# Mixer projections as three fp32r products of parted weights, and the first tile of a wide expert in plain fp32

## The chip, the cores and the metric

The kernel runs on one core of a Trainium2 chip. The metric is the device time of one execution in microseconds, lower is better; a time given for the kernel is the median of its runs. A core has TensorE (PE, matrix products), VectorE (DVE), ScalarE (ACT), GpSimd (POOL) and SyncE (SP), each with a queue of its own that is worked off in order, and 16 DMA engines that they share.

## The reference

Two layers over 256 tokens of width 1024, all in fp32. Each layer has two sub-layers, and each of these is a norm with a modulation by the condition vector (shift, scale and gate, three rows of 1024, from `silu(c) @ w_ada`), the sub-layer itself, a second norm, and the gated addition to x.

```python
h = rmsnorm(x, g_norm[l, 0]) * (1.0 + scale) + shift
# hybrid_mixer: one input projection, three head groups, one output projection
(q1, q2, k1, k2, va, qb, kb, vb, ob, ib, fb, cq, ckv, kr) = split(h @ w_in)      # 1024 x 2668
out_a = diff_attention_group(q1, q2, k1, k2, va, ...)                           # 4 heads
out_b = mlstm_group(qb, kb, vb, ob, ib, fb, ...)                                # 6 heads
out_c = mla_group(cq, ckv, kr, ...)                                             # 6 heads
y = concatenate([out_a, out_b, out_c]) @ w_out                                  # 1024 x 1024
x = x + gate * rmsnorm(y, g_norm[l, 1])
...
# layer 0: dense SwiGLU of width 3584; layer 1: 8 experts of that width, each token goes to 2
y = (silu(h @ w_gate) * (h @ w_up)) @ w_down
```

## The kernel before

It is written as one instruction stream for each engine, with semaphores between them by hand; nothing is scheduled by a planner. The stages are mixer 0, dense MLP, mixer 1, and the eight experts one after another.

**Weights.** All weights but the experts' stand in one list, `weight_uses()`, in the order of use: for each mixer 12 input projection items (`W_IN_ORDER`: two for the latents of group c with the gates, then a0, a1, va, qk0, qk1, qk2, ob0, ob1, and two for vb), thirds of a modulation as four quarters each (`ADA_MIXER`), and four output projection items (`OUT_ORDER`, columns 2, 3, 0, 1). A use is up to 1 MB, 128 partitions by 2048 elements. SyncE loads use u (L756) into slot u mod 7 of `ring`, and waits for that with the last reader of use u-7 (`last_reader`), so at most seven uses are in flight or in use. TensorE waits for the landing.

**Mixer on TensorE.** Every input projection is a plain fp32 product, of h (`hT`, feature-major) with the landed weight: `fm_pair` (L949) makes two feature-major banks of 128 rows by 256 tokens with 16 products of 256 columns, `tm` (L957) makes the token-major latents, va and vb. `ada_rows` (L866) multiplies a third's four quarters with the condition vector in 32 products, and waits for all four; `ada_columns` (L877) turns the result. Between the projections stand the attention units. Behind vb come, in this order: the turns `pt`, the modulation rows of the mixer's second last third, the gates (L1144), mt0, the pairs of units w and s of the mLSTM group (L1162, L1170; ScalarE takes the exponential of w, VectorE multiplies), co (L1185), bo (L1199), mt1 and mt2, the output projection's early feature tiles (L1211, `MIX_EARLY`) for two column groups, the modulation rows of the last third, mt3 and mt4, and the rest of the output projection. All of it takes its mixed rows from `mixT`.

**Dense MLP and experts.** These use three fp32r products in place of one fp32 product: the weight's high part (ScalarE Copy to fp32r, `parts<-ring`), its low part (VectorE, weight minus high part), and the same for h; high x high, high x low and low x high are added up in PSUM. Experts have a ring of their own of 14 slots of 1 MB (SyncE, L762), 42 uses each. An expert's code is chosen by its count of rows: up to 64 narrow (plain fp32, L1370 and L1382), 128 split, 160 or 192 wide. Here two are wide, one of 160 and one of 192 rows. `expert_wide` has 14 stages; a stage multiplies two inner tiles' gate and up weights in two halves (`gate_up_half`: L1414 with high weights and high and low rows side by side, L1420 with low weights), adds and multiplies them on ScalarE and VectorE (L2403, L2406), and a stage later the down projection (L1433, L1442). ScalarE copies the high parts of the first weights once it has the expert (L1563, `scr_parts<-ring`); VectorE makes the rows' high and low part (L2392, L2394) and the weights' low parts (L2365).

All ScalarE instructions are recorded under the one helper line, L1563.

Of the kernel before, what the change touches and what calls it, by code (L numbers as in the profile page):

```python
# [24 lines left out]
P = 128  # L25
# [91 lines left out]
def weight_uses():  # L117
# [6 lines left out]
    def w_in(l, a, b):  # L124
        uses.extend(("in", l, key) for key in W_IN_ORDER[a:b])

    def mixer(l):
# [6 lines left out]
        uses.extend(("out", l, c) for c in OUT_ORDER)  # L134
# [27 lines left out]
def pack_weights(inputs):  # L162

    def cols(w, c, n):
        return w[:, c:c + n].reshape(KD, P, n).transpose(1, 0, 2).reshape(-1)
# [5 lines left out]
    for kind, a, b in weight_uses():  # L171
        if kind == "ada":
            parts.append(cols(inputs["w_ada"][a // 2, a % 2], b * SW, SW))
        elif kind == "in":
# [10 lines left out]
def pack_experts(inputs):  # L185
# [15 lines left out]
W_IN_ORDER = [(COL_LAT, 256), (COL_LAT + 256, LATW - 256), (COL_Q, 256), (COL_Q + 256, 256), (COL_VA, 256),  # L201
              (COL_QK, 256), (COL_QK + 256, 256), (COL_QK + 512, 256), (COL_OB, 256), (COL_OB + 256, 128),
              (COL_VB, 256), (COL_VB + 256, 128)]
# [20 lines left out]
            *[f"pt{u}" for u in range(6)], "rows2", "gt", "mt0", "cols2", "co0", "co1", "mt1", "mt2", "rows3",  # L224
# [64 lines left out]
def build(nc, ap, out, ypairs):  # L289
# [13 lines left out]
    with ExitStack() as ctx:  # L303
# [172 lines left out]
        yeK = hT.rearrange("p k t -> p (k t)").rearrange("p (b d) -> p b d", b=TB)  # L476
        htok_hi, htok_lo = (h_parts[:, i, :, :].rearrange("p k t -> p (k t)").rearrange("p (b d) -> p b d", b=TB) for i in range(2))
# [81 lines left out]
        tok_ready = sem("tok_ready")  # L559
        split_hi = sem("split_hi")  # L560
# [66 lines left out]
        def use_wait(eng, u):  # L627

            eng.wait_ge(landed[slot_of[u]], 16 * (u // SLOTS + 1))
# [98 lines left out]
        def _(sp):  # L728
            def last_reader(kind, a, b):

                if kind == "ada":
                    return tr_full, TR.full(("ada", a, b // 4))
                if kind == "in":
                    return pj_full, PJ.full((IN_ITEM[b], a))
                if kind == "out":
                    return (y_full, 2 + a) if b == OUT_ORDER[-1] else (out_read, (D // SW - 1) * a + OUT_ORDER.index(b) + 1)
                return split_lo, dense_use(kind, b) + 1

# [4 lines left out]
            for u, (kind, a, b) in enumerate(uses):  # L743
                if u >= SLOTS:
                    sp.wait_ge(*last_reader(*uses[u - SLOTS]))
                n = KD * (b[1] if kind == "in" else SW)
                slot = ring[:, slot_of[u], :, :]
                if n < KD * SW:
                    slot = slot[:, :, 0:n // KD]
# [45 lines left out]
        def _(pe):  # L795
# [605 lines left out]
            def expert_wide(e, n):  # L1401
# [55 lines left out]
                for s in range(STAGES + 1):  # L1457
# [4 lines left out]
                    if s:  # L1462
                        down_rest(s - 1)
# [1131 lines left out]
```

## Time and profile before

| | |
|---|---|
| median of 3 runs | 1719.91 us (1714.5 to 1721.17) |
| profiled execution | 1717.92 us |
| its span | 1716.1 us |
| mean granted TensorE clock | 0.95 |
| TensorE busy | 1512.4 us, 88% |
| VectorE busy | 732.0 us, 43% |
| ScalarE busy | 561.5 us, 33% |
| GpSimd busy | 63.2 us, 4% |
| bytes moved | 488.85 MB, 285 GB/s |

The span is what the profile shows from first to last instruction; the time has 1.8 us more around it. TensorE busy includes time in which it works at half its clock. The mixers stand at about 28 to 216 and 481 to 667 us, the dense MLP between them, the experts from about 706 on.

### The profile page before, as it was taken

The numbers are of one execution on the slowest core, as the hardware profiler recorded it, in microseconds if no ns is written. First come the engines' busy times: TensorE is split into PE (matmuls) and PEld (weight loads), VectorE is DVE, ScalarE is ACT, GpSimd is POOL, SyncE is SP. The second block draws the span as 40 slices with busy tenths as digits, with TensorE's granted clock in tenths as the row PEclk, the third lists the DMA queues.
The fourth block names the chain that finished last, engine by engine and source line by source line (L and its number), as shares of the span: only waits on it lengthen the run. The fifth ranks groups of instructions, "written<-read, shape, count | busy, mean of one in ns | idle before, by whom it ended". The sixth has DMA issues, their size and how long they took to land.

```text
span 1716.1 us, 29819 instructions
## 1 busy us (share of the span) xinstructions
PE 1512.4 (88%) x12054; PEld 1200.4 (70%) x12055; DVE 732.0 (43%) x1058; ACT 561.5 (33%) x777; POOL 63.2 (4%) x66
## 2 busy tenths in 40 slices
PE   5999999999999999856659999989997669999894
PEld 3868878999976776644447875489995458888552
DVE  2263265565534522300018871166772036666212
ACT  2134144444322321100016751056551035554101
POOL 0010000000010001000000000000000000000002
PEclk9999999999999999987879999989999779999997
DMA  9726467545352436699999999997577996555793
GB/s 357 273 95 239 191 245 276 201 176 203 138 192 74 173 147 274 273 424 423 425 425 426 400 378 403 425 369 286 236 279 313 424 424 260 221 221 221 311 426 149
DMA packets 74557, 488.85 MB, mean 285 GB/s; under 512 B 9792, under 2 KB 13920, under 8 KB 16544
## 3 DMA queue, kind: packets, MB, share of 16 engines
q1 hardware_dynamic: 72176, 479.94, 69.7%
q10 hardware_dynamic: 1648, 4.59, 0.8%
q8 instruction: 114, 1.87, 0.4%
q0 software_dynamic: 576, 2.10, 0.4%
q14 instruction: 43, 0.35, 0.1%
HBM read 482.66 MB, written 3.93 MB: 284 GB/s over the span
## 4 chain that ended last, share of the span: by engine, by line
PE 79%; DMA 10%; issue 5%; DVE 3%; ACT 2%; POOL 1%; SPq 1%; ACTq 0%; POOLq 0%; DVEq 0%
PE PG L1370 9%; PE PG L923 6%; PE Y L949 5%; PE PG L1414 5%; PE PG L1480 5%; PE TRB L1414 4%; DMA arena<-in_experts 4%; PE Y L1382 4%; PE Y L1442 4%; DMA ring<-in_experts 4%; PE Y L1211 3%; PE Y L957 3%; PE PG L925 3%; PE TRB L1420 3%; PE PG L1420 3%
## 5 line engine op out<-in xcount | busy, mean ns | idle before, releaser
L1370 PE MATMUL PG<-ring,mixT 128*32 128x128 f32 (+1 forms) x1920 | 116.3, 347 | 61.4 <-issue 56.9
L2381 DVE COPY arena<-TRB 128x64 f32<-128x64 f32 (+1 forms) x70 | 17.6, 251 | 340.3 <-PE TRB L1356 340.3
L1563 ACT ACTIVATE parts<-ring 128x2048 fp32r<-128x2048 f32 x84 | 157.2, 1901 | 4.8 <-PE PG L1480 4.8
L923 PE MATMUL PG<-h_parts,parts 128*128 128x512 f32 x432 | 152.8, 394 | 1.4 <-DVE arena L2260 1.4
L1370 PEld LDWEIGHTS PG<-ring,mixT 128*32 128x32 f32 (+1 forms) x1920 | 89.5, 136 | 91.7 <-issue 77.0
L1563 ACT ACTIVATE rope<-PG 64x128 f32<-64x128 f32 (+2 forms) x84 | 27.2, 324 | 376.5 <-PE PG L1370 352.6
L1370 PE MATMUL PG<-arena,mixT 128*32 128x128 f32 (+1 forms) x1664 | 103.6, 357 | 41.3 <-issue 41.3
L1370 PEld LDWEIGHTS PG<-arena,mixT 128*32 128x32 f32 (+1 forms) x1664 | 79.8, 141 | 69.1 <-issue 55.1
L925 PE MATMUL PG<-h_parts,parts 128*128 128x256 f32 x432 | 121.8, 282 | 0.0
L2245 DVE TENSOR_TENSOR parts<-ring,parts 128x2048 fp32r<-128x2048 f32 x42 | 95.1, 2289 | 32.7 <-ACT parts L1563 32.7
L2365 DVE TENSOR_TENSOR ring_parts<-ring,parts 128x2048 fp32r<-128x2048 f32 x42 | 95.0, 2286 | 22.4 <-PE Y L1433 19.4
L2365 DVE TENSOR_TENSOR parts<-arena,parts 128x2048 fp32r<-128x2048 f32 x42 | 95.2, 2287 | 17.6 <-PE Y L1433 14.9
L923 PEld LDWEIGHTS PG<-h_parts,parts 128*128 128x128 f32 x432 | 81.2, 188 | 19.4 <-DVE arena L2260 1.6
L949 PE MATMUL Y<-hT,ring 128*128 128x256 f32 x416 | 93.2, 384 | 0.0
L949 PEld LDWEIGHTS Y<-hT,ring 128*128 128x128 f32 x416 | 79.4, 193 | 11.6 <-issue 0.8
L925 PEld LDWEIGHTS PG<-h_parts,parts 128*128 128x128 f32 x432 | 81.3, 188 | 0.0
L1563 ACT ACTIVATE parts<-arena 128x2048 fp32r<-128x2048 f32 x42 | 78.9, 1901 | 3.6 <-PE PG L1480 3.6
L890 PE MATMUL Y<-parts 128*128 128x256 f32 x224 | 63.4, 283 | 0.2 <-DVE parts L2269 0.2
L892 PE MATMUL Y<-parts 128*128 128x256 f32 x224 | 63.4, 283 | 0.0
L891 PE MATMUL Y<-parts 128*128 128x256 f32 x224 | 63.4, 283 | 0.0
L1414 PEld LDWEIGHTS PG<-h_parts,scr_parts 128*128 128x128 f32 x224 | 37.3, 198 | 36.3 <-ACT scr_parts L1563 20.4
L1414 PE MATMUL PG<-h_parts,scr_parts 128*128 128x320 f32 (+1 forms) x224 | 45.7, 348 | 19.0 <-ACT scr_parts L1563 19.0
(358 smaller groups left out, 2715.6 us busy)
## 6 DMA issues: line engine op xcount, KB each, us to landing
ring<-in_experts SPq DMA_DIRECT2D x168, 1024.0 KB, 12.2
arena<-in_experts SPq DMA_DIRECT2D x168, 1024.0 KB, 16.3
ring<-in_weights SPq DMA_DIRECT2D x116, 1024.0 KB, 6.3
ring<-in_weights SPq DMA_DIRECT2D x4, 512.0 KB, 4.2
ypairs<-hT ACTq DMA_DIRECT2D x3, 512.0 KB, 5.4
tok<-in_x SPq DMA_DIRECT2D x1, 1024.0 KB, 9.0
result<-scr SPq DMA_DIRECT2D x2, 512.0 KB, 2.6
ring<-in_weights SPq DMA_DIRECT2D x2, 432.0 KB, 6.5
```

The lines of the kernel that those rows point to most:

```text
L923: mm(PG[:, m, :].rearrange("p (i t) -> p i t", i=2), w_hi[d % SPLITS][:, c], h_parts[:, :, k, :], start=(k == 0), stop=False, skip_group_c ...
L925: last = mm(PG[:, m, 0:T], w_lo[d % SPLITS][:, c], h_hi[:, k, :], start=False, stop=(k == KD - 1), skip_group_check=True)
L949: last = mm(bank_part, ring[:, s, k, c:c + m], hT[:, k, :], start=(k == 0), stop=(k == KD - 1))
L1370: last = mm(bank[i * n:(i + 1) * n, 0:width], xe[:, k, 0:n], w[k // 4][:, k % 4, i * width:(i + 1) * width], start=(k == 0), stop=(k == KD ...
L1382: last = mm(o, actT[:, s % 2, f, 0:n], w[:, f, c:c + width], start=(s == 0 and f == 0), stop=(s == STAGES - 1 and f == 1))
L1414: last = mm(both, hi[:, k, i // 2, i % 2, :], h_parts[:, :, h * KD // 2 + k, 0:n], start=(h == 0 and k == 0), stop=False, skip_group_check ...
L1420: last = mm(bank[:, 0:n], lo[:, k, i // 2, i % 2, :], h_parts[:, 0, h * KD // 2 + k, 0:n], start=False, stop=(h == 1 and k == KD // 2 - 1) ...
L1442: last = mm(o, a[:, s % 2, f, :], w[:, f, c:c + width], start=(opens and s == 0 and f == 0), stop=(closes and s == STAGES - 1 and f == 1))
L1480: last = mm(bank, x[j][:, h * KD // 2 + k, :], w[:, k, :], start=(opens and k == 0), stop=(closes and k == KD // 2 - 1))
L1563: return nc.scalar.activation(out_, in_, func, **kw)
L2245: V.tensor_tensor(w_lo[d % SPLITS], ring[:, slot_of[slot_of_dense(d)], :, :].rearrange("p k c -> p (k c)"), w_hi[d % SPLITS].bitcast(F32), ...
L2365: V.tensor_tensor(w_lo_e[q % SLOTS_E], ring_e[q % SLOTS_E].rearrange("p k c -> p (k c)"), w_hi_e[q % HI].bitcast(F32), ALU.subtract).then_ ...
```

## The change

In the mixers every projection weight is now parted: it takes two uses of the ring, the weight itself (`"in"`, `"out"`) and a place for its high part (`"hi"`), for which SyncE issues nothing. ScalarE copies the high part (`part`), VectorE subtracts it from the weight in place (`lower`). h goes to `h_hi`, its low part to `h_lo` (`low_shifted`). TensorE makes three products.

```diff
     def w_in(l, a, b):
-        uses.extend(("in", l, key) for key in W_IN_ORDER[a:b])
+        uses.extend((kind, l, key) for key in W_IN_ORDER[a:b] for kind in ("in", "hi"))
...
-        uses.extend(("out", l, c) for c in OUT_ORDER)
+        uses.extend((kind, l, c) for c in OUT_ORDER for kind in ("out", "hi"))
...
+            def part(l, key):
+                u, n = proj_use(l, key)
+                use_wait(ae, u)
+                if u + 1 >= SLOTS:
+                    ae.wait_ge(*last_reader(*uses[u + 1 - SLOTS]))
+                run(ring_parts[:, slot_of[u + 1], 0:n], ring[:, slot_of[u], :, :].rearrange("p k c -> p (k c)")[:, 0:n],
+                    ACT.Copy).then_inc(proj_hi, 1)
...
+            def lower(l, key):
+                u, n = proj_use(l, key)
+                ve.wait_ge(proj_hi, proj_index(l, key) + 1)
+                V.tensor_tensor(ring_parts[:, slot_of[u], 0:n], ring[:, slot_of[u], :, :].rearrange("p k c -> p (k c)")[:, 0:n],
+                                ring_parts[:, slot_of[u + 1], 0:n].bitcast(F32), ALU.subtract).then_inc(proj_lo, 1)
...
                 def fm_pair(name, key, n=2):
                     bank = take_pj((name, l))
-                    s = slot("in", key)
+                    hi, lo = proj_parts(l, key)
+                    hi_of(key)
                     for i in range(n):
-                        last = fm(bank[:, i * T:(i + 1) * T], s, i * P, P)
+                        for k in range(KD):
+                            for x in (h_hi, h_lo):
+                                mm(bank[:, i * T:(i + 1) * T], hi[:, k, i * P:(i + 1) * P], x[:, k, :],
+                                   start=(i == 0 and k == 0 and x is h_hi), stop=False, skip_group_check=True)
+                    lo_of(key)
+                    for i in range(n):
+                        for k in range(KD):
+                            last = mm(bank[:, i * T:(i + 1) * T], lo[:, k, i * P:(i + 1) * P], h_hi[:, k, :],
+                                      start=False, stop=(k == KD - 1), skip_group_check=True)
                     last.then_inc(pj_full, 1)
```

`latents` does the same for both latent items at once (48 products of 364 columns; each item is now half of the features, not of the columns), `tm` for va (256 columns) and vb (384 columns), `mixed` for the output projection. The mixed rows go to `mix_hi` and `mix_lo`. ScalarE's parts stand by hand between its other work: the first two between the two first modulation thirds, the first output weight's ahead of the w exponentials. The last third's modulation rows move from between the early and late output projection to behind co.

```diff
-                run(mixT[:, 0:2, :], bank.rearrange("p (a t) -> p a t", a=2), ACT.Copy, scale=gd[:, l:l + 1]).then_inc(free, 1)
+                run(mix_hi[:, 0:2, :], bank.rearrange("p (a t) -> p a t", a=2), ACT.Copy,
+                    scale=gd[:, l:l + 1]).then_inc(mix_hi_ready, 1)
+                part(l, OUT_ORDER[0])
                 ae.wait_ge(*tr_done("gt", l))
                 for h in range(BH):
...
             mean("pre", 0)
+            lower(0, W_IN_ORDER[0])
             for third in ADA_START:
                 ada(third)
...
+                part(l, W_IN_ORDER[10])
                 at(2)
                 at(3)
+                part(l, W_IN_ORDER[11])
```

In a wide expert the first stage's gate and up are multiplied in plain fp32 from the landed weights; their conversion is left out, and the rows' low part is made in two halves later.

```diff
+                def gate_up_whole():
+
+                    for h in range(2):
+                        w = landed_unit(e, "gu", 0, h).rearrange("p (k g f c) -> p k f g c", k=KD // 2, g=2, f=2)
+                        for i, bank in enumerate(banks):
+                            for k in range(KD // 2):
+                                last = mm(bank[:, 0:n], w[:, k, i // 2, i % 2, :], xe[:, h * KD // 2 + k, 0:n],
+                                          start=(h == 0 and k == 0), stop=(h == 1 and k == KD // 2 - 1))
+                            if i == 2:
+                                used = last
+                        (used if h else last).then_inc(hi_used, 1)
+                    last.then_inc(gu_full, 2)
...
-                for q in range(HI):
-                    weights_lo(e, q)
+                ve.sem_inc(conv_lo, 2)
+                weights_lo(e, expert_at["gu", 1, 0])
                 for s in range(STAGES):
                     if s == 0:
+                        ve.wait_ge(hi_used, e * USES + 1)
+                        low_rows_of(0)
                         weights_lo(e, expert_at["gu", 1, 1])
```

SyncE's queue in layer 0's mixer, before: the rows from the last vb weight on, each with the kind of reader that it waits for (`pj_full` a projection, `tr_full` modulation rows or turns, `out_read` and `y_full` the output projection).

```order
13 L756 DMA ring<-in_weights 128x8x128 [waits tr_full]
14 L756 DMA ring<-in_weights 128x2048 [waits tr_full] x3
15 L756 DMA ring<-in_weights 128x2048 [waits pj_full] x4
16 L756 DMA ring<-in_weights 128x2048 [waits tr_full] x8
17 L756 DMA ring<-in_weights 128x2048 [waits out_read] x3
18 L756 DMA ring<-in_weights 128x2048 [waits y_full]
```

The same place now, from the two vb halves (128x1536) on:

```order
12 L781 DMA ring<-in_weights 128x1536 [waits tr_full] x2
13 L781 DMA ring<-in_weights 128x2048 [waits pj_full] x7
14 L781 DMA ring<-in_weights 128x2048 [waits tr_full] x5
15 L781 DMA ring<-in_weights 128x2048 [waits out_read] x5
16 L781 DMA ring<-in_weights 128x2048 [waits y_full] x2
```

Before, row 13 is the last vb weight. Three quarters of the modulation third behind vb (row 14) wait for the modulation rows ahead of ob, its fourth for ob0; the next third's first quarter waits for ob1 and the next two for vb (row 15); its last and three output weights wait for the modulation rows behind vb. Now the seven loads behind vb are that third's four quarters and three of the next third's: the first three wait for ob, the other four for vb. The eighth and the first output weight wait for the modulation rows behind vb.

ScalarE in layer 0, before: from the modulation rows behind vb to the first w exponentials (`arena<-PG,aK`).

```order
74 L1563 ACTIVATE arow<-TRB 128x256 [waits tr_full]
75 L1563 ACTIVATE aK<-TRB 128x12 [waits tr_full]
76 L1563 ACTIVATE em<-TRB 128x12
77 L1563 ACTIVATE mixT<-TRB,gd 128x512 [waits tr_full]
78 L1563 ACTIVATE arena<-PG,aK 128x256 [waits sc_full,tr_free1]
79 L1563 ACTIVATE arena<-PG,aK 128x128
```

The same place now:

```order
87 L1653 ACTIVATE arow<-TRB 128x256 [waits tr_full]
88 L1653 ACTIVATE aK<-TRB 128x12 [waits tr_full]
89 L1653 ACTIVATE em<-TRB 128x12
90 L1653 ACTIVATE h_parts<-TRB,gd 128x512 [waits tr_full]
91 L1653 ACTIVATE ring_parts<-ring 128x2048 [waits tr_full,landed6]
92 L1653 ACTIVATE arena<-PG,aK 128x256 [waits sc_full,tr_free1]
93 L1653 ACTIVATE arena<-PG,aK 128x128
```

Row 91 is new: the part of the first output weight, with a wait for its landing (slot 6), ahead of all exponentials.

TensorE at the start of the wide expert of 160 rows, before:

```order
2633 L1456 ISA [waits xe_ready]
2634 L1396 ISA [waits x_split]
2635 L1414 MATMUL PG<-h_parts,scr_parts 128x320 [waits conv_hi]
2636 L1414 MATMUL PG<-h_parts,scr_parts 128x320 x7
2637 L1414 MATMUL TRB<-h_parts,scr_parts 128x320 x8
2638 L1420 MATMUL PG<-h_parts,ring_parts 128x160 [waits conv_lo]
```

The same place now:

```order
2840 L1420 ISA [waits xe_ready]
2841 L1489 MATMUL PG<-mixT,ring 128x160 [waits landed_e0]
2842 L1489 MATMUL PG<-mixT,ring 128x160 x7
2843 L1489 MATMUL TRB<-mixT,ring 128x160 x8
2844 L1489 MATMUL PG<-mixT,ring 128x160 [waits landed_e1]
2845 L1489 MATMUL PG<-mixT,ring 128x160 x7
2846 L1489 MATMUL TRB<-mixT,ring 128x160 x8
2847 L1550 ISA
2848 L1551 ISA [waits act_ready]
2849 L1474 ISA [waits x_split]
2850 L1505 MATMUL PG<-h_parts,parts 128x320 [waits conv_hi]
```

The first products wait for landings where they waited for the conversion (`conv_hi`); the second stage's are the first that need it.

## Rows read from the trace of the kernel before

**Rows 1.** The page, part 4: the chain that ended last, by engine.

```profile
PE 79%; DMA 10%; issue 5%; DVE 3%; ACT 2%; POOL 1%; SPq 1%; ACTq 0%; POOLq 0%; DVEq 0%
```

**Rows 2.** Windows: stretch, us, busy PE PEld DVE ACT POOL, TensorE clock, DMA share, GB/s.

```profile
40.00:216.00 176.00, 171.68 (x1090) 134.26 (x1092) 64.92 (x151) 49.75 (x129) 11.57 (x8) 1.00 0.52 201
1143.00:1290.00 147.00, 147.00 (x1111) 132.79 (x1111) 101.67 (x84) 83.48 (x85) 0.27 (x1) 1.00 0.66 262
1290.00:1375.00 85.00, 57.93 (x1071) 42.92 (x1069) 12.16 (x33) 9.07 (x22) 1.63 (x1) 0.86 0.94 383
```

**Rows 3.** Timeline of layer 0's projections, TensorE: start, busy time, line, operation [idle before].

```profile
40.21 10.70 PE L957 MATMUL Y<-ring,hT 128*128 128x256 f32 x64 [1.38 <-ACT hT L1563]
50.74 13.99 PE L949 MATMUL Y<-hT,ring 128*128 128x256 f32 x64
150.88 5.40 PE L957 MATMUL Y<-ring,hT 128*128 128x256 f32 x32
```

**Rows 4.** Timeline of TensorE in the dense MLP and expert 6: single fp32r products.

```profile
245.69 0.28 PE L890 MATMUL Y<-parts 128*128 128x256 f32 x1
247.95 0.28 PE L891 MATMUL Y<-parts 128*128 128x256 f32 x1
1400.80 1.59 PE L1414 MATMUL PG<-h_parts,parts 128*128 128x384 f32 x8
1402.22 1.57 PE L1414 MATMUL TRB<-h_parts,parts 128*128 128x384 f32 x8
```

**Rows 5.** The page, part 5: turning 128x2048 weights into parts, ScalarE and VectorE.

```profile
L1563 ACT ACTIVATE parts<-ring 128x2048 fp32r<-128x2048 f32 x84 | 157.2, 1901 | 4.8 <-PE PG L1480 4.8
L2245 DVE TENSOR_TENSOR parts<-ring,parts 128x2048 fp32r<-128x2048 f32 x42 | 95.1, 2289 | 32.7 <-ACT parts L1563 32.7
```

**Rows 6.** Timeline of layer 0's mixer behind its last vb projection.

```profile
158.31 3.66 PE L866 MATMUL TRB<-ring,ccol 128*32 128x256 f32 x64
164.05 1.44 ACT L1563 ACTIVATE arena<-PG,aK 128x256 f32<-128x256 f32 x4
170.92 4.13 PE L1185 MATMUL TRB<-arena 128*128 128x64 f32 x36
180.64 8.87 PE L1211 MATMUL Y<-mixT,ring 128*128 128x256 f32 x40 [0.90 <-ACT mixT L1563]
195.16 12.32 PE L1211 MATMUL Y<-mixT,ring 128*128 128x256 f32 x56
215.09 1.38 PE L833 MATMUL TRB<-scr,ones 128*32 128x256 f32 x8
```

**Rows 7.** Tile ring, 156 to 170: the issues, and their time to landing.

```profile
L756 SPq DMA_DIRECT2D ring<-in_weights x6: 327/432/732, 156.3 to 163.4; - x6
DMA to landing us min/median/max: 4.9/7.1/12.3
```

**Rows 8.** Timeline of layer 0's first modulation rows, and a window inside them.

```profile
32.17 5.35 PE L866 MATMUL TRB<-ring,ccol 128*32 128x256 f32 x64 [2.22 <-DMA ring<-in_weights]
33.00:36.00 3.00, 3.00 (x35) 1.91 (x28) 0.00 (x0) 0.00 (x0) 0.00 (x0) 0.50 1.09 343
```

**Rows 9.** Timeline of the first wide expert's start (160 rows), and its first loads.

```profile
1108.32 3.65 PE L1382 MATMUL Y<-arena 128*64 128x512 f32 x16
1117.26 1.91 ACT L1563 ACTIVATE scr_parts<-ring 128x2048 fp32r<-128x2048 f32 x1
1119.22 2.50 PE L1414 MATMUL PG<-h_parts,scr_parts 128*128 128x320 f32 x8 [7.25 <-ACT scr_parts L1563]
1132.33 2.49 PE L1414 MATMUL PG<-h_parts,parts 128*128 128x320 f32 x8 [1.85 <-DVE rope L2403]
ring<-in_experts SPq DMA_DIRECT2D x2, 1024.0 KB, 19.7
```

**Rows 10.** Timeline of the second wide expert's start (192 rows).

```profile
1394.31 2.93 PE L1414 MATMUL PG<-h_parts,scr_parts 128*128 128x384 f32 x8 [11.79 <-ACT scr_parts L1563]
1407.65 2.17 PE L1414 MATMUL PG<-h_parts,parts 128*128 128x384 f32 x8 [2.09 <-DVE rope L2403]
```

More of the change, by code:

```diff
@@ L173, in pack_weights @@
             parts.append(cols(inputs["w_ada"][a // 2, a % 2], b * SW, SW))
+        elif kind == "hi":
+            continue
+        elif kind == "in" and b in K_HALF:
+            at, n, k = K_HALF[b]
+            parts.append(cols(inputs["w_in"][a], at, n, k, KD // 2))
         elif kind == "in":
@@ new lines, in tm @@
+                def tm(bank_part, b, his, los):
+                    for k in range(KD):
+                        nk = KD // len(his)
+                        x_hi, x_lo = (x[:, k, b * P:(b + 1) * P] for x in (h_hi, h_lo))
+                        mm(bank_part, x_hi, his[k // nk][:, k % nk, :], start=(k == 0), stop=False, skip_group_check=True)
+                        mm(bank_part, x_lo, his[k // nk][:, k % nk, :], start=False, stop=False, skip_group_check=True)
+                    for k in range(KD):
+                        last = mm(bank_part, h_hi[:, k, b * P:(b + 1) * P], los[k // nk][:, k % nk, :],
+                                  start=False, stop=(k == KD - 1), skip_group_check=True)
@@ L1014, in mixer @@
                 keys = W_IN_ORDER
-                s0, s1 = slot("in", keys[0]), slot("in", keys[1])
-                for b in range(TB):
-                    bank = take_pj((f"lat{b}", l))
-                    tm(bank[:, 0:SW], s0, b, SW, first=(b == 0))
-                    last = tm(bank[:, SW:LATW], s1, b, LATW - SW)
-                    last.then_inc(pj_full, 1)
+                latents()
                 fm_pair("a0", keys[2])
@@ L1207, in mixed, with product @@
                 def mixed(c, tiles):
-                    s = slot("out", c)
+                    hi, lo = proj_parts(l, c)
+                    late = tiles is MIX_LATE
+                    def product(w, x, k, j):
+                        return mm(Yk[:, 2 * c + j, :], w[:, k, j * P:(j + 1) * P], x[:, k, :],
+                                  start=(j == 0 and k == 0 and w is hi and x is mix_hi),
+                                  stop=(late and k == MIX_LATE[-1] and x is mix_lo), skip_group_check=True)
+                    hi_of(c)
                     for j in range(2):
                         for k in tiles:
-                            last = mm(Yk[:, 2 * c + j, :], ring[:, s, k, j * P:(j + 1) * P], mixT[:, k, :],
-                                      start=(j == 0 and k == 0), stop=(k == MIX_LATE[-1]), skip_group_check=True)
+                            product(hi, mix_hi, k, j)
+                    if not late:
+                        for j in range(2):
+                            for k in tiles:
+                                product(hi, mix_lo, k, j)
+                    lo_of(c)
+                    for j in range(2):
+                        for k in tiles:
+                            last = product(lo, mix_hi, k, j)
+                    if late:
+                        pe.wait_ge(mix_lo_ready, 2 * l + 2)
+                        for j in range(2):
+                            for k in tiles:
+                                last = product(hi, mix_lo, k, j)
                     return last
@@ L1731, in _ @@
             run(cos[CN:CN + CR, :], cos[CN:CN + CR, :], ACT.Sin).then_inc(rope_set, 1)
-            for third in ADA_START:
-                ada_rows(third)
+            ada_rows(ADA_START[0])
+            for key in W_IN_ORDER[0:2]:
+                part(0, key)
+            ada_rows(ADA_START[1])
             shift(0)
@@ L1772, in _ @@
             load_latent_weights(1)
+            for key in W_IN_ORDER[0:2]:
+                part(1, key)
             squares_pre(2)
```

264 lines of the change are left out of this document (181 added, 83 removed).

## The prediction

> **What bounds the kernel now.** I read the chain of waits first, to see on which engine the end hangs, then the windows, since the answer is not the same in every stage. 79% of the chain is TensorE, 10% transfers [rows 1]. In the windows the reader is to see three kinds of stage: layer 0's mixer, where TensorE is busy 171.68 of 176 us with half of the DMA share in use; the first wide expert's stages, busy 147.00 of 147 us; and a narrow expert, 57.93 of 85 us with the DMA engines at 0.94 [rows 2]. Both parts of the change lie on the bound: the projections in the first kind, the start of a wide expert ahead of the second. So TensorE time saved there is time saved at the end, as long as no new wait takes it back.
>
> **The projections, before the last vb (point V).** Four feature-major banks of 16 fp32 products take the 64 matmul records from 50.74 to 64.58 for two pairs, so 13.84/2 = 6.92 us a pair (the busy 13.99 counts a modelled tail), 0.433 a product of 256 columns [rows 3]. An fp32r product of 256 columns costs (247.95 - 245.69)/19 = 0.119 us, one of 384 columns (1402.22 - 1400.80)/8 = 0.178 [rows 4]. Three products in place of one make a pair 48 x 0.119 = 5.71: 1.21 less. There are six such items (a0, a1, va, qk0 to qk2), ob0 as well, ob1 at half, and two vb of 24 x 0.178 = 4.26 against about 5.3 (the row's 5.40 less its tail). Sum: 7 x 1.21 + 0.6 + 2 x 1.05 = 11.2 us a layer. The latents' 10.70 [rows 3] become 48 products of 364 columns, about 0.17 each, the first eight at the pace at which h comes: 0.8 less.
>
> What is added is conversion: every weight is copied on ScalarE (1.90 us) and subtracted on VectorE (2.29 us) [rows 5], 4.2 us behind its landing, and each takes two of the seven slots. Both engines have the room (64.92 and 49.75 us of 176 busy [rows 2]), so I cost most of it at nothing; a pair's 5.71 us on TensorE covers the pair of conversions of the next. Where they stand in line with something urgent they cost: a half of the latents (1456 of 2048 columns, 1.35 us on ScalarE) stands ahead of the copy of the modulation rows, +1.3; at2 and at3 stand behind the part of a vb weight, +1.9; the first vb product waits for its second low part (1.6 on ScalarE, 1.7 on VectorE less what lies beside at and pt), +2.1; pt1, +0.3. V comes 11.2 + 0.8 - 5.6 = 6.4 us earlier in layer 0, I take 6.6 with rounding of the hand walk. In layer 1 the two latent parts stand ahead of squares and means that the norm needs, +2.0, with the rest as above: V 5.6 earlier.
>
> **From V to the end of the output projection (E).** Before, V is about 156.1, the modulation rows of the second third run at 158.31, the first exponentials at 164.05, the c outputs at 170.92, the early part of the output projection at 180.64, the late part at 195.16, E at 215.09: 59.0 us [rows 6]. Here the lookahead decides. The SP order shows that the seven loads ahead of the last third's last quarter wait for projections: the last quarter of that third is now released by V itself, and behind it come the other third's four quarters and the output weights. A lone 1 MB lands 4.9 us after its issue, and a train of them comes at 2.5 us each (the row's 4.9, 7.1, then up to 12.3) [rows 7]. Issued at V they land at V+5.1, 7.6, 10.2, 12.7, then 15.3, and the first output weight, sixth in that train, at V+17.8. ScalarE's order has the high part of that weight ahead of the w exponentials, which before ran at V+7.9. They now start at 17.8 + 1.9 = V+19.8: a block of 11.9 us in which TensorE has next to nothing. w and s take 6.9 (164.05 to 170.92), so c begins at V+26.3, where it was V+14.8; the modulation rows (3.66) and bo follow to V+37.9, the early output part starts at V+40.5 (before V+24.5) and takes 60 x 0.119 = 7.15 for 8.8, since the modulation rows between early and late are gone. The late part has its inputs at V+50.1 and takes (36 + 96) x 0.119 = 15.7, plus 0.6 for the statistics and 1.1 for the low parts of the mixed rows: E = V+67.5, so +8.5 a layer. Bounds of the block: nothing, if the weight were there in time (E = V+55.6, a gain of 3.4), or 14.4 us, if each of the five loads between takes 3 us (12.3 us for the last of a train is the nearest row). I keep 11.9, since the order of the queue leaves little choice.
>
> **The clock.** A pause of 2.22 us ends with a granted clock of 0.50, which is 1.2 of 2.4 GHz, and 64 modulation matmuls that take 3.66 us elsewhere take 5.35: 1.7 us lost a time [rows 6, 8]. The change makes about three such pauses in each layer (before the last quarter, before w, before the output part). The rival price is 0, if TensorE has little to do in that time anyway (w and s are paced by ScalarE and VectorE), the other end 6. I take 4 a layer, 8 in all.
> The Trainium skill speaks against this change here: "TensorE: Matmul & The Clock Gate", section "HAM oscillation — how this bites in real kernels", says that a loop whose bursts of matmuls are parted by waits for transfers pays for the clock anew at every wait. By that rule each of the six pauses costs its 1.7, so 10 in place of my 8, and the forecast 1724. The trace agrees with it for the one pause in front of the modulation rows.
>
> **The wide experts.** Before, TensorE ends the expert before at 1112.0 (1108.32 + 3.65), waits for ScalarE's high part (1117.26 for 1.91) and starts at 1119.22, after 7.25 idle; the second tile starts at 1132.33 [rows 9]. With the landed weights (issued at about 1090, 19.7 to landing, so 1110 and 2 us later) the first tile is 32 fp32 products of 160 columns, 0.433 x 160/256 = 0.270 each, 8.6 us: done at 1120.7, no conversion in front. Then VectorE sets the pace: its own high rows, the low part of the third weight (ScalarE 1117.26 to 1119.15, then 2.29), half the low rows, the low part of the fourth, two copies: 1125.4, where TensorE takes up the second tile. That is 6.9 before 1132.33; I take 6.5. In the second wide expert TensorE comes only at about 1389.9, from fetching its code (11.79 idle up to 1394.31, the rest of it for ScalarE) [rows 10]; 32 x 0.324 = 10.4 plus the slow clock 2, plus copies: 1403.9 for 1407.65, 3.8, and 0.7 for the shorter pause in front of the next tile: 4.5. What is won is kept: the stages behind are TensorE's alone, and the narrow expert's transfers are released by TensorE's progress, so they shift with it. Together -11, between -5 (VectorE's chain longer by two more conversions, the copies behind them) and -16 (no pause at all, full clock).
>
> **Sum** against the profiled execution, 1717.92 us (span 1716.1): -6.6 - 5.6 + 17.0 + 8 - 11 + 0.3 (a third's rows behind the later landing) = +2.1, 1720.0. The median of the runs is 1719.91, 2 us over that execution, so I forecast 1722.
>
> **The rivals.** A, faster: before V the conversions run wholly beside TensorE. For it: the two engines are busy a third of the time, and the ring lets them work a weight ahead [rows 2]; against it: their orders put attention's copies behind parts that wait for a landing. Then V moves by the whole 12.0 in each layer, and fewer pauses leave 4 of the clock's 8: -24 + 17 + 4 - 11 = -14, and 1706. It would be 1683 with the block gone as well, to which I give nothing apart from the range's edge, since the block follows from the queue's order. B, slower: the block, and the clock at 0.50 throughout w, s, c and the early output part. It decides from the point where TensorE's bursts there are too thin to bring the clock back: the 11.9 us block then costs 4 to 5 more a layer (some 9 us of TensorE work at double time, half hidden), and the wide expert's fp32 tile at half clock gives back 6 of the 11. 1722 + 9 + 6 = 1737.
> ScalarE's engine queue is strict first in, first out by the Trainium skill ("TensorE: Matmul & The Clock Gate", section "Architectural detail: the array is 16× 32×32, not 1× 128×128"), so by it nothing behind the waiting part can pass it, and no row here shows a pass.
> C: the experts' part does nothing, since the wide tile's start is bound by the landing and the code fetch: 1722 + 11 = 1733. For it speaks that at the first wide start DMA is full, against it that its weights land before TensorE comes.
>
> **How the numbers follow.** Forecast 0.38 (own range 1712 to 1730), A 0.29, B 0.25, C 0.08. A measurement of this kernel tells 0.5% (8.6 us) from no change. Of the forecast's share a twentieth falls on either side of 1711.3 and 1728.5, and of A's and C's a little within them. Faster 0.29, same 0.37, slower 0.34. The range takes in A's and B's prices: 1701 to 1739.
>
> **What would show it.** In each mixer, an idle of TensorE in front of w of 8 to 12 us, ended by ScalarE, itself waiting for a landing; the c outputs about V+26; the output projection's records at 0.119 us; V at about 149.5 in layer 0; granted clock 0.50 around V+20. For the experts: fp32 records of 160 columns from 1112 on, relative to the end of the expert before, and the next tile 13 us behind. The forecast is wrong if the first output weight lands before V+10, if the low parts (VectorE) hold the pairs before V, or if the windows of w and s show the clock at 1.00.

## The result and the profile after

The changed kernel takes 1729.47 us in the median of 7 runs (1727.48 to 1735.51), beside 1719.39 us for the kernel before: a ratio of 1.0066, 95% interval [1.0049, 1.0083]. It is slower by 0.5 to 0.8%, 8 to 14 us. The profiled execution took 1727.48 us, its span 1725.7 us, 9.6 more than before.

The first view is TensorE's timeline of layer 0's mixer, which answers to [rows 3] and [rows 6]; columns as there.

```profile
41.72 5.52 PE L1001 MATMUL Y<-ring_parts,h_parts 128*128 128x364 f32 x16 [1.39 <-ACT h_parts L1653]
52.30 4.09 PE L979 MATMUL Y<-h_parts,ring_parts 128*128 128x256 f32 x32
...
134.69 4.63 PE L1179 MATMUL TRB<-arena 128*128 128x64 f32 x24 [1.34 <-ACT arena L1653]
...
139.71 0.52 PE L1023 MATMUL Y<-ring_parts,h_parts 128*128 128x384 f32 x1
...
147.82 0.34 PE L1022 MATMUL Y<-ring_parts,h_parts 128*128 128x384 f32 x1
...
152.01 1.30 PE L1069 MATMUL TRB<-con,arena 128*128 128x128 f32 x8
...
157.16 6.42 PE L891 MATMUL TRB<-ring,ccol 128*32 128x256 f32 x64 [2.89 <-DMA ring<-in_weights]
...
173.54 1.65 PE L1221 MATMUL PG<-arena,con 128*128 128x384 f32 x2 [6.36 <-ACT arena L1653]
...
180.38 4.13 PE L1244 MATMUL TRB<-arena 128*128 128x64 f32 x36
...
194.68 7.42 PE L1272 MATMUL Y<-h_parts,ring_parts 128*128 128x256 f32 x60 [1.75 <-DVE h_parts L2306]
...
205.48 10.31 PE L1272 MATMUL Y<-h_parts,ring_parts 128*128 128x256 f32 x84
...
222.23 1.38 PE L858 MATMUL TRB<-scr,ones 128*32 128x256 f32 x8
```

The last vb product ends at 152.0 (V), 4.1 us earlier than before. The reader is to see one bracket ahead of it and three behind. Ahead: 1.34 us for ScalarE in front of at2, then 24 products in 4.63 us, and vb products of 384 columns at 0.32 us from start to start where the later ones take 0.17 (the windows 135 to 139 and 139 to 142 have a granted clock of 0.56 and 0.50). Behind: 2.89 us for the last quarter of a modulation third, whose rows then take 6.42 us in place of 3.66; 6.36 us for ScalarE in front of the second w pair; 1.75 us for VectorE. The output projection ends (E) at 222.2: 70.2 us behind V where it was 59.0. In layer 1 V comes at 611.1 and E at 683.3, 72.2 us:

```profile
596.98 0.66 PE L1022 MATMUL Y<-ring_parts,h_parts 128*128 128x384 f32 x1 [1.69 <-DVE ring_parts L2098]
...
616.22 5.35 PE L891 MATMUL TRB<-ring,ccol 128*32 128x256 f32 x64 [2.86 <-DMA ring<-in_weights]
...
632.78 1.65 PE L1221 MATMUL Y<-arena,con 128*128 128x384 f32 x2 [7.62 <-ACT arena L1653]
...
654.68 8.77 PE L1272 MATMUL Y<-h_parts,ring_parts 128*128 128x256 f32 x60 [1.80 <-DVE h_parts L2306]
```

What ScalarE does in layer 0's pause of 6.36 us stands in its own timeline:

```profile
164.84 0.69 ACT L1653 ACTIVATE h_parts<-TRB,gd 128x512 fp32r<-128x512 f32 x1 [0.63 <-PE TRB L1210]
170.95 1.91 ACT L1653 ACTIVATE ring_parts<-ring 128x2048 fp32r<-128x2048 f32 x1 [5.43 <-DMA ring<-in_weights]
172.77 1.34 ACT L1653 ACTIVATE arena<-PG,aK 128x256 f32<-128x256 f32 x4
```

It waits 5.43 us for the first output weight's landing, copies it, and only then takes the exponentials whose products had stood in PSUM since 165. The windows of the same stretch (stretch, us, busy PE, PEld, DVE, ACT, POOL, granted clock, DMA share, GB/s) show what the pauses do to the clock:

```profile
157.00:164.00 7.00, 6.76 (x68) 3.60 (x68) 0.00 (x0) 0.36 (x2) 0.00 (x0) 0.59 0.96 404
167.00:173.00 6.00, 0.17 (x4) 0.00 (x0) 0.00 (x0) 2.05 (x2) 0.00 (x0) 0.72 0.95 403
173.00:178.00 5.00, 4.46 (x17) 2.75 (x17) 3.68 (x4) 2.57 (x8) 0.00 (x0) 0.65 0.00 0
178.00:192.00 14.00, 14.00 (x152) 11.55 (x151) 4.65 (x9) 3.65 (x6) 0.00 (x0) 1.00 0.21 70
```

The wide experts' starts, which answer to [rows 9, 10], in TensorE's timeline:

```profile
1130.57 2.44 PE L1489 MATMUL PG<-mixT,ring 128*128 128x160 f32 x16 [2.97 <-issue]
...
1141.16 1.44 PE L1505 MATMUL PG<-h_parts,parts 128*128 128x320 f32 x8 [1.64 <-DVE rope L2583]
...
1403.31 5.48 PE L1489 MATMUL PG<-mixT,ring 128*128 128x192 f32 x16 [11.19 <-issue]
```

In the first, the second tile starts at 1141.16. Everything had been moved by 15.6 us there (the last narrow products start at 1123.94, before at 1108.32), so it is 6.8 us earlier than before relative to them. That holds for this execution. In a second profiled one of the same kernel (e10) the pause in front of the first tile is longer and the tile starts at half clock, the second tile starts at 1143.59 with the last narrow products at 1122.11, and only 2.5 us are gained:

```profile
1130.93 4.63 PE L1489 MATMUL PG<-mixT,ring 128*128 128x160 f32 x16 [5.16 <-issue]
```

In the second wide expert TensorE is idle for 11.19 us, and the profile shows nothing that it waits for ("issue"). I read this as the wait for its own code; the runs e6 to e12 bear on that.

GpSimd's copy of each expert's rows marks the experts' starts, so their differences are the time of an expert (us; of the last, up to the copy of the results):

```
                        start e0   e0     e1      e2     e3   e4 wide 160  e5   e6 wide 192  e7
before                    704.1   77.0   107.2   131.1   85.9    184.3    89.0    209.9    100.2
changed                   720.9   77.3   107.2   131.1   84.6    176.1    91.2    209.0    101.1
e1_wide_only              705.9   76.0   106.8   129.9   86.2    177.3    90.2    203.8    100.3
e2_mixer_only             719.9   75.4   108.6   129.9   84.4    181.6    91.5    210.8    100.3
```

So the 9.6 us are: layer 0's mixer +7.1 (the same products of the dense MLP stand at 247.1 for 240.0), layer 1's +9.7, the experts -7.2. One row is one execution: in e10, the changed kernel again, the wide expert of 160 rows takes 180.4 us and not 176.1.

### The profile page after: what moved, and what is told of

Read it like the earlier page. It is cut to its first block, busy times and chain, and to the rows that moved or that the text cites. A ratio compares the mean times of both kernels' runs of the same rounds, so it can differ in the third digit from the quotient of the medians.

```text
span 1725.7 us, 30580 instructions
## 1 busy us (share of the span) xinstructions
PE 1492.7 (86%) x12358; PEld 1197.5 (69%) x12359; DVE 801.1 (46%) x1120; ACT 603.9 (35%) x801; POOL 65.4 (4%) x66
## 4 chain that ended last, share of the span: by engine, by line
PE 44%; DMA 8%; issue 5%; DVE 2%; ACT 1%; POOL 1%; SPq 0%; ACTq 0%; POOLq 0%; DVEq 0%
PE PG L1448 9%; DMA ring<-in_experts 5%; PE PG L1570 5%; PE Y L1460 4%; PE PG L1505 4%; PE Y L1533 4%; PE TRB L1505 4%; PE TRB L1511 3%; PE PG L1511 3%; DMA arena<-in_experts 3%; PE Y L1601 2%; PE Y L1524 2%; PE TRB L1434 2%; PE Y L1272 1%; PE PG L1489 1%
## 5 line engine op out<-in xcount | busy, mean ns | idle before, releaser
L1653 ACT ACTIVATE parts<-ring 128x2048 fp32r<-128x2048 f32 x82 | 153.6, 1901 | 9.4 <-PE PG L1570 4.7
L1448 PE MATMUL PG<-arena,mixT 128*32 128x128 f32 (+1 forms) x1664 | 99.0, 339 | 37.1 <-issue 37.1
L1448 PEld LDWEIGHTS PG<-arena,mixT 128*32 128x32 f32 (+1 forms) x1664 | 75.4, 133 | 65.8 <-issue 51.8
L2536 DVE TENSOR_TENSOR ring_parts<-ring,parts 128x2048 fp32r<-128x2048 f32 x40 | 90.6, 2288 | 25.5 <-PE Y L1524 16.6
L2098 DVE TENSOR_TENSOR ring_parts<-ring,ring_parts 128x2048 fp32r<-128x2048 f32 (+3 forms) x32 | 66.4, 2077 | 37.7 <-ACT ring_parts L1653 37.6
L1653 ACT ACTIVATE ring_parts<-ring 128x2048 fp32r<-128x2048 f32 (+3 forms) x32 | 55.5, 1738 | 57.1 <-DMA ring<-in_weights 30.9
L891 PE MATMUL TRB<-ring,ccol 128*32 128x256 f32 x768 | 52.6, 435 | 10.5 <-DMA ring<-in_weights 10.5
L1460 PE MATMUL Y<-arena 128*32 128x256 f32 (+1 forms) x512 | 59.7, 458 | 1.9 <-issue 1.8
```

The source lines that it names most:

```text
L1448: last = mm(bank[i * n:(i + 1) * n, 0:width], xe[:, k, 0:n], w[k // 4][:, k % 4, i * width:(i + 1) * width], start=(k == 0), stop=(k == KD ...
L1460: last = mm(o, actT[:, s % 2, f, 0:n], w[:, f, c:c + width], start=(s == 0 and f == 0), stop=(s == STAGES - 1 and f == 1))
L1653: return nc.scalar.activation(out_, in_, func, **kw)
L2098: V.tensor_tensor(ring_parts[:, slot_of[u], 0:n], ring[:, slot_of[u], :, :].rearrange("p k c -> p (k c)")[:, 0:n], ring_parts[:, slot_of[u ...
L2536: V.tensor_tensor(w_lo_e[q % SLOTS_E], ring_e[q % SLOTS_E].rearrange("p k c -> p (k c)"), w_hi_e[q % HI].bitcast(F32), ALU.subtract).then_ ...
```

## The experiments

Ratios are to the kernel before on the same chip, with their 95% intervals.

```
kernel                  median us   ratio, interval            V to E, layers 0 and 1
before                  1719.39                                59.0   59.0
changed                 1729.47     1.0066 [1.0049, 1.0083]    70.2   72.2
e1_wide_only            1706.77     0.9936 [0.9920, 0.9951]
e2_mixer_only           1736.55     1.0110 [1.0095, 1.0124]
e3_part_behind          1712.42     0.9962 [0.9949, 0.9976]    63.6   60.9
e4_rows_behind          1701.88     0.9897 [0.9882, 0.9913]    56.9   56.7
e5_tuned                1700.49     0.9889 [0.9869, 0.9910]    57.5   57.3
e6_shift_a (2 runs)     1697.46     0.9877 [0.9848, 0.9905]
e7_shift_b (2 runs)     1698.71     0.9884 [0.9864, 0.9904]
e8_after_shift          1727.96     1.0063 [1.0043, 1.0084]
e9_tuned_shift          1702.39     0.9916 [0.9893, 0.9938]
```

e10, e11 and e12 are the changed kernel, e1 and e9 once more, one execution each: 1731.22, 1709.15 and 1704.00 us, beside one of 1713.28 us for the kernel before.

**e1_wide_only and e2_mixer_only: the two parts of the change, each alone.** e1 has the edits of `expert_wide` on the kernel before, e2 is the changed kernel with `expert_wide` as before. Of e1's edit two lines:

```diff
+                gate_up_whole()
+                for s in range(1, STAGES + 1):
```

> The wide experts' part alone, the mixers as before. Theory 1 (the two parts add up, and the experts' part gains what the two traces show): the span is 7.2 us shorter than before, 8 at the first wide expert, 1 at the second, and 2 of it given back in the narrow one between them: 1711 to 1713 us. Theory 2 (the gain is an accident of when the transfers stand, since the mixers moved all loads by 17 us): anything from 1705, if the second wide expert gains its 4.5, to 1720.

> The mixers' part alone, the experts as before. Theory 1 (parts add up): 7 us in layer 0 and 9.7 in layer 1 more than before, 16.8 in all, 1735 to 1738 us, with all experts later by the same 16.8. Rival: the experts' transfers, released later, take up part of the shift: under 1733.

The experts' part gains 0.64% by itself, 11.0 us, more than theory 1 allowed (1706.8 us for 1711 to 1713); the mixers' part loses 1.1%, 18.9 us, as forecast. From mixers alone to both is 0.44%, 7.6 us. So the parts do not quite add up: with the new mixers the wide experts' part brings 3 to 4 us less. The table of experts shows where, each part beside its own base: with the old mixers the first wide expert gains 7.0 us (184.3 to 177.3) and the second 6.1 (209.9 to 203.8), with the new ones 5.5 (181.6 to 176.1) and 1.8 (210.8 to 209.0). The second is the larger loss; the first varies by 4 us between executions.

**e3_part_behind: the copy that waits for a landing moved behind the exponentials.**

```diff
-                part(l, OUT_ORDER[0])
                 ae.wait_ge(*tr_done("gt", l))
                 for h in range(BH):
...
+                part(l, OUT_ORDER[0])
                 ada_rows(ADA_MIXER[l][3])
# VectorE: lower(l, OUT_ORDER[0]) from "if h == 2" to behind the c outputs
```

> The changed kernel with one part moved: ScalarE copies the first output weight behind the w exponentials, and VectorE subtracts it behind the c outputs. Theory 1 (head of line: the copy that waits for a landing holds exponentials that wait for nothing): the pause of 6.4 us in front of the second w pair goes in both layers, with it some 2 us of slow clock: 8 to 10 a layer, 16 to 19 in all, so 1710 to 1714 us, under the kernel before; the output projection starts 8 to 10 us earlier behind the last vb. Rival (the transfers are the limit: the next output weights and the modulation rows are late anyway): the pause moves to the modulation rows behind the c outputs or to the output projection, and the time stays at 1726 to 1730.

From 1.0066 to 0.9962: 1.0%, 18 us, by the place of one instruction on two engines. TensorE's timeline of layer 0, V at 151.6:

```profile
156.78 6.43 PE L891 MATMUL TRB<-ring,ccol 128*32 128x256 f32 x64 [2.89 <-DMA ring<-in_weights]
...
164.27 0.81 PE L1221 MATMUL PG<-arena,con 128*128 128x384 f32 x2
...
172.16 4.13 PE L1244 MATMUL TRB<-arena 128*128 128x64 f32 x36
...
186.45 8.88 PE L1272 MATMUL Y<-h_parts,ring_parts 128*128 128x256 f32 x60 [1.75 <-DVE h_parts L2305]
```

w and s now stand without a pause, the c outputs come at V+20.5 (V+28.4 in the changed kernel), and no later wait took the pause's place. V to E is 6.6 us shorter in layer 0 and 11.3 in layer 1, together the 18. The wait for the quarter is as in the changed kernel.

**e4_rows_behind: those modulation rows behind two pairs of w and s.**

```diff
-            "rows2", "gt", "mt0", "cols2", "co0", ...
+            "gt", "mt0", "rows2", "cols2", "co0", ...
...
                 for h0 in range(0, BH, 2):
+                    if h0 == 4:
+                        ada_rows(ADA_MIXER[l][2])
# ScalarE: ada_rows(ADA_MIXER[l][2]) at h == 4 of its loop
```

> As e3_part_behind, and the modulation rows behind vb (the third whose last quarter is issued only when vb is done) moved on TensorE and ScalarE from in front of the gates to between the second and third pair of w and s. Theory 1: they waited 2.9 us for the landing and then ran at half clock (6.4 us for 3.7), 5.6 us a layer; behind two pairs (V+9) the quarter (landed V+5.1) is there and the clock holds: 11 us less than e3_part_behind, 1701 to 1703 us. Rival: what comes behind it is late in its place (the next third's last quarter and the first output weight are issued when these rows end, 3.5 us later than before): the c outputs' modulation rows or the output projection wait, and 1708 to 1712.

```profile
161.47 3.66 PE L891 MATMUL TRB<-ring,ccol 128*32 128x256 f32 x64
```

No wait in front, 3.66 us: full clock. V to E falls to 56.9 and 56.7 us, below the 59.0 of the kernel before, and the ratio by 0.65%, some 11 us, to 0.9897. The rival, a late output weight in front of the output projection, did not come. Its mechanism shows one step later: behind E in layer 0 the next norm's modulation rows wait 2.72 us for their landing and run at half clock (0.34 us and full clock in e3), and from E to the dense MLP it is 18.9 us for e3's 16.5. The experts' part alone stands at 0.9936, so of e4's 1.0% under the kernel before some 0.4% are the mixers', if the parts add up.

**e5_tuned: three smaller waits out.**

```diff
-            for key in W_IN_ORDER[0:2]:
-                part(0, key)
-            ada_rows(ADA_START[1])
+            part(0, W_IN_ORDER[0])
+            ada_rows(ADA_START[1])
+            part(0, W_IN_ORDER[1])
...
# TensorE, mixed(): high x high, low x high, then high x low rows, with the wait for these
# ada_columns(ADA_MIXER[l][3]) behind the late products of the first two column groups
```

> As e4_rows_behind, with three more waits taken out: the second latent weight's high part behind the copy of the modulation row (1.4 us, layer 0 alone), the output projection's products with the mixed rows' low parts last (1.75 us a layer and its slow clock 1.5), and the last third's columns turned behind the first late products (2.25 us a layer). Theory 1: 1.4 + 2 x 5.5 = 12 us less than e4: 1689 to 1692 us. Rival: VectorE, whose order stays, is late next, with the low parts of the late mixed rows and of the output weights: 1694 to 1698.

The forecast of 12 us was wrong: 1 us, within the intervals. The rival's mechanism is in the timeline:

```profile
180.05 7.44 PE L1273 MATMUL Y<-h_parts,ring_parts 128*128 128x256 f32 x60 [0.74 <-ACT h_parts L1652]
188.54 0.88 PE L1209 MATMUL TRB<-con,hT 128*128 128x128 f32 x6 [1.04 <-DVE hT L2330]
190.88 5.87 PE L1273 MATMUL Y<-h_parts,ring_parts 128*128 128x256 f32 x36 [1.47 <-DVE h_parts L2336]
...
216.79 5.35 PE L891 MATMUL TRB<-ring,ccol 128*32 128x256 f32 x64 [2.81 <-DMA ring<-in_weights]
```

The output projection starts earlier, and waits for VectorE's normed rows and late mixed rows instead; what is left of it waits for the next norm's modulation weights, at half clock behind that.

**e6 to e12: the pause before the second wide expert.** The edit puts `t` one-element products on TensorE into the routing and takes some filler products out, so that all expert code stands further on.

```diff
-            busy(xg_banks[0], 4)
+            busy(xg_banks[0], b)
+            for _ in range(t):
+                mm(xg_banks[0][0:1, 0:1], con[:, 0:1], con[:, 0:1], start=True, stop=True)
# on e5_tuned: e6 b 4, t 16; e7 b 1, t 35; e9 b 3, t 17; e8 as e9, on the changed kernel
```

> As e5_tuned, with 16 one-element products more on TensorE in the routing, which shift all expert code by 64 instructions if each fp32 product is four. Open is why TensorE comes to the second wide expert 11.2 to 12.6 us after its last product in every kernel with the new mixers, and after 7.1 to 7.4 us in the two with the old ones. Theory A (where the expert's code stands in the program's pages decides how many are fetched): the pause changes by more than 2 us for one of the two shifts, the rest of the kernel stays. Theory B (it depends on where the transfers stand, or on other code): it stays at 11 to 12.6 us in both. Time 1 to 2 us over e5_tuned, less what the pause gives.

> As e6_shift_a with twice the shift: three of the filler products of the routing less, 35 one-element products more. Theory A: the pause in front of the second wide expert is 7 to 8 us in this one or in e6_shift_a, and the second wide expert then gains the 6 us that it gained with the old mixers. Theory B: 11 to 12.6 us.

> The changed kernel itself, its expert code shifted by 64 instructions with one-element products on TensorE in the routing, nothing else. Theory 1 (the experts' part missed 4 to 5 us of its gain for where the code stands): the pause before the second wide expert falls from 11.2 to about 7 us, that expert from 209 to 204, the whole by 4 to 6 us: 1723 to 1726. Rival (the pause hides other waits, for landings): the pause is shorter and the next wait longer, 1728 to 1731.

> e5_tuned with the same shift, one filler product of the routing less to make room for it: the version that the runs point to. 1694 to 1698 us, 4 to 6 below e5_tuned and some 21 below the kernel before. Rival: what e6_shift_a showed in one round was chance, and it stays at 1699 to 1702.

> The changed kernel once more, for one look. Open is whether the pause before the second wide expert (11.2 us here, 7.1 in e1_wide_only, 12.2 and 8.9 in the two last kernels with shifted code) belongs to a kernel or to an execution. Theory A (a kernel's own): 11 to 12.6 us again. Theory B (an execution's own, from how the code's packets fall among the weights'): it may be 7 to 9 us, and the second wide expert then 204 to 206 us.

> The wide experts' part alone once more, for one look. Theory A: pause of 7.1 us and 204 us for the second wide expert again. Theory B: it may be 11 to 12 us and 209.

> e9_tuned_shift once more, for one look. Theory A: 8.9 us again. Theory B: anything from 7 to 12.6.

TensorE's idle in front of its first product there, and the time of that expert (us):

```
                     pause   expert                            pause   expert
e1_wide_only          7.1    203.8      e2_mixer_only          12.6    210.8
e11 (e1 again)        7.2    204.8      changed                11.2    209.0
e6_shift_a            7.0    204.2      e10 (changed again)    11.4    208.8
e7_shift_b            7.1    204.8      e8_after_shift         12.2    210.3
e9_tuned_shift        8.9    205.6      e3, e4, e5        11.9, 11.6, 11.9    209.2, 208.8, 209.6
e12 (e9 again)        8.4    206.1
```

The row of e1 that answers to the changed kernel's at 1403.31, whose idle was 11.19:

```profile
1383.12 4.38 PE L1411 MATMUL PG<-mixT,ring 128*128 128x192 f32 x16 [7.12 <-issue]
```

This pause went with the kernel and not with the execution in all three that were run again, within 0.5 us, and 4 us of pause are 4 to 5 us of the expert. The pause before the first wide expert did not: 2.97 us in the changed kernel and 5.16 in e10. What the pause is made of stands in the view of the transfers, which has queues of the kind "instruction" (packets, MB, share). The changed kernel, 1392.1 to 1403.3:

```profile
q8 instruction: 3, 0.05, 2.0%
q14 instruction: 3, 0.02, 0.6%
```

e1_wide_only, 1376 to 1383.1:

```profile
q8 instruction: 2, 0.03, 2.1%
q14 instruction: 2, 0.02, 0.6%
```

In every trace of a pause of 7.0 to 8.9 us q8 has two packets in it (e1, e11, e6, e7, e9, e12), in every trace of one of 11.2 to 12.6 us three (changed, e10, e2, e3, e4, e5, e8). So the pause is long where one more packet of code falls into it. The trace does not say whose code it is. Two shifts of the code took e5_tuned's from 11.9 to 7; a third of nearly the same length to 8.9; and the changed kernel's rose from 11.2 to 12.2. So the place of the code matters, but the plain rule that I tried (a given shift gives a given pause) is refuted, and what decides between two packets and three, and between 7.0 and 8.9 us at two, is open. Taking filler products out (e7, e8, e9) is a second change in the same edit and was not tested by itself. Both forecasts built on that rule missed: e8 was to take 1723 to 1726 us and took 1728.0, e9 1694 to 1698 and took 1702.4. In e8 the time did not fall clearly below the changed kernel's, in e9 not below e5_tuned's (the intervals overlap), so none of it is a version to prefer. The best that is shown is e4_rows_behind or e5_tuned, 1.0 to 1.1% under the kernel before.

## Why the prediction was right where it was, and where it missed

It said 1722, 1712 to 1730 in the likeliest case, 1701 to 1739 in all. The measured 1729.5 lies at the upper end of the likeliest case. It is slower by 0.66%, just more than the 0.5% that I had named as the least that can be told from no change; I had given 0.34 to slower and 0.37 to the same, so the forecast did not name the direction. The gap of 7.5 us comes from two of the terms, V (4.5) and the experts (3.8). In spans:

- **Before V, forecast -6.6 and -5.6, measured -4.1 and -3.6: 4.5 us too much.** The pace of the products was right (from a0 to the modulation rows 17.46 us for 20.84: -3.4, forecast 3 x 1.21; the same again up to the next rows, -3.3). The latents did not gain their 0.8: their first 16 products take as long as h's parts come (41.72 for 5.52), and 10.58 us up to a0 stand beside 10.53. The start is 1.5 us later for 1.3. The stretch with at2, at3 and vb is +1.0 over the old one where I had some +0.4, but that nearness is luck: two terms were wrong in opposite ways. Of the waits that I had (1.9 for at2 and at3, 2.1 for vb's second low part) layer 0 shows 1.5 and nothing. In their place stands half clock behind the pause of 1.34 us, which I had not priced before V at all: at's 24 products take 4.63 us for 2.79, and the first vb item 5.68 (139.25 to 144.93) where at full clock the second takes 4.19, together some 3.4 us. In layer 1 vb does wait, 1.69 us, and the item behind it takes 7.05 us. The row of before for at's products:

```profile
140.07 2.79 PE L1122 MATMUL TRB<-arena 128*128 128x64 f32 x24
```

- **From V to E, forecast +8.5 and 4 for the clock, 12.5 a layer; measured +11.2 and +13.2.** The step that carried the sum was right in place, engine and total size: w's exponentials at V+20.8 (forecast V+19.8), c outputs V+28.4 (26.3 without the clock; by its own terms the forecast should say 19.8 + 6.9 = 26.7), TensorE idle and ended by ScalarE, ScalarE ended by a landing. e3 shows it as a cause. The forecast's own signs are only in part there: the idle in front of w is 6.4 and 7.6 us where it said 8 to 12, and stands in front of the second pair of w; the granted clock from 170.95 to 172.8 (V+19 to V+20.8) is 0.50 as it said; V is at 152.0, not 149.5. One link was wrong: the first output weight was not the sixth in a train. The modulation rows ended at 163.5, and it was the second of the loads issued then (163.6, 164.0, 164.5), landed 6.9 us after its issue, near the middle value of [rows 7], 7.1. The train that I counted had been through before; instead, the wait of 2.89 us for the last quarter and the rows at half clock (6.42 for 3.66) delayed the release. That the landing came at V+18.9 where I had V+17.8 is luck: another link had nearly the same length. Layer 1 takes 2.0 us more than layer 0, with a longer idle (7.62 for 6.36) and more lost to the clock.
- **The clock, forecast 4 a layer:** 2.8 in the modulation rows (6.42 less 3.66) and 1.4 in the second w pair (173.54 to 177.53, 3.99 us, beside 2.57 for the same pair before, 165.50 to 168.07): 4.2 in layer 0. In layer 1 it is 1.7, 2.1 (632.78 to 637.49, beside 2.58) and 1.4 in the early output projection: 5.2. The half clock before V, 3.4 in layer 0 and some 2.8 in layer 1, comes on top, so a layer lost 7.6 to 8 us to the clock where the forecast had 4; the part before V is hidden in the term V above. The Trainium skill's rule on waits between bursts ("TensorE: Matmul & The Clock Gate", "HAM oscillation — how this bites in real kernels") is borne out by the pauses in front of the modulation rows and the second w pair; behind the third, the 60 products ran at full pace in layer 0 (1.75 us of pause, 7.42 us) and not in layer 1 (1.80 us, 8.77 us).
- **The experts, forecast -11, measured -7.2 in the changed kernel and -11.0 alone (e1).** The first wide start was right in the profiled execution (6.8 us for 6.5; the next tile's clock gave 1.4 more), with some luck: nine other traces with this start show 5.6 to 6.8, e10 and e3 2.5. In the second I had TensorE arrive 7 us behind its last product, as in the kernel before; in the changed kernel it arrives after 11.2. My rows could not show that cost; one more packet of code goes with it.

Rival A (the waits before V vanish) and B (half clock throughout w, s, c and the output projection) did not happen: V moved by 4.1 and 3.6 for A's 12.0, and of B's stretch only the second w pair ran slow (0.65 from 173 to 178), while the window 178 to 192 has a clock of 1.00. C is refuted by e1. The 0.3 for a norm's modulation rows did not show: E and the dense MLP's start are later by the same 7.1.

## What to carry to other kernels

An instruction that waits for a transfer belongs in an engine's order behind all work that is ready, whatever its place in the data's order: here one copy ahead of the w exponentials cost 18 us of 1729, more than twice what the faster products won before V in both layers (4.1 and 3.6 us). When each weight takes two slots of a ring, walk the releases from the ring's length, since the lookahead halves and the last use before a phase change sets the first of the next; then put the work that needs it behind something that does not. Test the two halves of a double change apart: one gained 0.64%, the other lost 1.1%, and the sum looked like little.

## What the runs showed of the hardware

- At the branch to the second wide expert, with the DMA engines at a share of 1.0, TensorE was idle for 7.0 to 8.9 us in some kernels and 11.2 to 12.6 in others with the same block. The three kernels that were run again kept it within 0.5 us. The short pauses have two packets of queue q8 (kind "instruction") in them, the long ones three, and 16 tiny products far ahead took it from 11.9 us to 7.0 (e5, e6). The pause before the first wide expert is not as steady (2.97 and 5.16 us in two executions of the changed kernel).
- A pause of TensorE in front of the 64 modulation products was followed by a stretch at half clock in all 28 cases of the traces with a pause of 2.0 to 4.2 us: 5.06 to 6.56 us for 3.66, a price of 1.4 to 2.9 us, most often 1.7 (the changed kernel's 2.89 and 2.86 us gave 6.42 and 5.35). In the seven cases with 0.2 to 1.7 us they took 3.66. The length of the pause alone does not decide it: behind the 1.34 us in front of at2 the clock fell to 0.50 in layer 0 (4.63 us for the 24 products), and behind 1.33 us in layer 1 it did not (2.86).
- fp32r products of 256 columns came at 0.124 us in the output projection (48 from 216.29 to 222.23), beside 0.119 in the dense MLP [rows 4].
